# Sums over channels with six blocks added ahead, the gated norm's coefficient on ScalarE, gated blocks in pairs, and a result in four transfers

## The reference, cut to what matters

```
def layer_norm(x, g, b):                     # first block, four times
    mu = mean(x); var = mean(square(x - mu))
    return (x - mu) * rsqrt(var + 1e-5) * g + b

def rmsnorm(u, g):                           # second block
    return u * rsqrt(mean(u * u) + 1e-6) * g

x = layer_norm(ALPHA * x + mix, ln1_g, ln1_b)              # first block
x = layer_norm(ALPHA * x + mlp(x), ln2_g, ln2_b)
xl_new = xl + ml[2] * rmsnorm(y_l, g_post_mix)             # second block, "gated" norm after the mixer
xl_new = xl_new + ml[5] * rmsnorm(mlp_2(h2), g_post_mlp)   # and after the MLP
```

## Time and profile before

| what | value |
| --- | --- |
| median of 3 runs | 1805.22 us (1800.21 to 1808.81) |
| the profiled execution, its own time | 1801.04 us |
| its span, first to last instruction | 1799.2 us |
| outside the span | 1.84 us |
| mean granted TensorE clock | 0.976 |
| TensorE (PE) busy | 1647.6 us, 92% |
| VectorE (DVE) busy | 1190.9 us, 66% |
| ScalarE (ACT) busy | 536.0 us, 30% |
| GpSimd (POOL) busy | 375.8 us, 21% |
| bytes moved | 247.27 MB, mean 137 GB/s |

### The profile page before, as it was taken

How to read it: one execution, slowest core, us unless ns; L and a number is a source line. 1 busy time by engine, 2 the same in 40 slices (tenths; PEclk the granted TensorE clock), 3 DMA queues, 4 the chain that set the end, 5 groups by cost and what they waited for, 6 DMA issues and landing times.

```text
span 1799.2 us, 26861 instructions
## 1 busy us (share of the span) xinstructions
PE 1647.6 (92%) x10914; PEld 1420.9 (79%) x10914; DVE 1190.9 (66%) x1662; ACT 536.0 (30%) x1062; POOL 375.8 (21%) x308
## 2 busy tenths in 40 slices
PE   7978599999899999999888999999999798889996
PEld 6867489999688999988645578888888475679996
DVE  6653478888866888859764464444444687478886
ACT  4424231111353122143465340101011545641111
POOL 1100124444112444400000111212122000134442
PEclk9989899999999999999999999999999899999998
DMA  7850655565656555542201313233333140235551
GB/s 292 296 202 11 235 188 177 187 187 177 235 186 222 176 176 178 180 168 94 82 1 33 132 59 105 90 97 93 98 92 102 37 151 24 70 93 177 176 175 46
DMA packets 69875, 247.27 MB, mean 137 GB/s; under 512 B 7456, under 2 KB 10528, under 8 KB 69664
## 3 DMA queue, kind: packets, MB, share of 16 engines
q1 hardware_dynamic: 69792, 246.18, 42.5%
HBM read 245.10 MB, written 1.05 MB: 137 GB/s over the span
## 4 chain that ended last, share of the span: by engine, by line
PE 64%; DVE 26%; ACT 8%; issue 2%; DMA 1%; SPq 0%; DVEq 0%; ACTq 0%
PE psum L352 14%; PE psum L354 14%; PE psum L353 14%; DVE lo_ring L317 8%; DVE relu L1158 4%; DVE hid_lo L1159 3%; PE psum L368 3%; PE psum L370 2%; PE psum L369 2%; PE psum L988 2%; DVE x L1121 1%; PE psum L451 1%; DVE normed L1119 1%; DVE c_soft L1807 1%; ACT c_p L1628 1%
## 5 line engine op out<-in xcount | busy, mean ns | idle before, releaser
L1965 POOL TENSOR_SCALAR hi_ring<-raw_ring 128x1024 fp32r<-128x1024 f32 x304 | 375.6, 1238 | 1396.5 <-PE psum L354 935.5
L317 DVE TENSOR_TENSOR lo_ring<-raw_ring,hi_ring 128x1024 fp32r<-128x1024 f32 x356 | 535.5, 1505 | 76.1 <-PE psum L354 30.9
L352 PE MATMUL psum<-x_hi,hi_ring 128*128 128x256 f32 (+1 forms) x1360 | 427.7, 315 | 24.9 <-DVE lo_ring L317 13.0
L353 PE MATMUL psum<-x_lo,hi_ring 128*128 128x256 f32 (+1 forms) x1360 | 422.2, 310 | 0.0
L354 PE MATMUL psum<-x_hi,lo_ring 128*128 128x256 f32 (+1 forms) x1360 | 422.1, 310 | 0.0
L352 PE MATMUL psum<-hid_hi,hi_ring 128*128 128x256 f32 (+1 forms) x1024 | 316.8, 309 | 4.1 <-DVE hid_lo L1159 4.1
L354 PE MATMUL psum<-hid_hi,lo_ring 128*128 128x256 f32 (+1 forms) x1024 | 314.6, 307 | 0.0
L353 PE MATMUL psum<-hid_lo,hi_ring 128*128 128x256 f32 (+1 forms) x1024 | 314.0, 307 | 0.0
L352 PEld LDWEIGHTS psum<-x_hi,hi_ring 128*128 128x128 f32 x1360 | 261.2, 192 | 48.8 <-DVE lo_ring L317 18.2
L353 PEld LDWEIGHTS psum<-x_lo,hi_ring 128*128 128x128 f32 x1360 | 261.4, 192 | 13.4 <-issue 0.2
L354 PEld LDWEIGHTS psum<-x_hi,lo_ring 128*128 128x128 f32 x1360 | 261.3, 192 | 13.1
(11 more groups left out here) (376 smaller groups left out, 1962.5 us busy)
## 6 DMA issues: line engine op xcount, KB each, us to landing
raw_ring<-weights SPq DMA_DIRECT2D x460, 512.0 KB, 3.9
h_const<-hyb_consts SPq DMA_DIRECT2D x1, 1088.0 KB, 11.7
x<-xT SPq DMA_DIRECT2D x1, 1024.0 KB, 5.9
x<-ctxT SPq DMA_DIRECT2D x1, 1024.0 KB, 17.1
outT<-x SPq DMA_DIRECT2D x1, 1024.0 KB, 4.8
shared<-shared_consts SPq DMA_DIRECT2D x1, 398.0 KB, 13.8
par<-params SPq DMA_DIRECT2D x1, 301.5 KB, 6.5
```

Of the source, the lines that this page charges most:

```text
L317: nc.vector.tensor_tensor(lo_ring[:, s, :], raw_ring[:, UNIT_AT[u] % RAW_SLOTS, :], hi_ring[:, s, :].bitcast(F32), ALU.subtract).then_inc( ...
L352: nc.tensor.matmul(bank(u % BANKS, T), w_hi, hi[:, k, 0:T], start=(k == 0), stop=False)
L353: nc.tensor.matmul(bank(u % BANKS, T), w_hi, lo[:, k, 0:T], start=False, stop=False)
L1965: nc.gpsimd.tensor_scalar(hi_ring[:, n % SPLIT_SLOTS, :], raw_ring[:, slot, :], 1.0, 0.0, ALU.mult, ALU.add).then_inc(hi_ready, 1)
```

## The change

Five edits. (1) `add_block`: while the last eight units of a stage are drained, VectorE adds blocks 0 to 5 of the tensor that will be summed (`y` for norms 0 to 3, `sq` for norms 5, 7, 9 and 11) into slot 1 of `normed`, one `tensor_tensor` for each of k = 1 to 5; for `sq` it runs one unit later. (2) `added_pe`: TensorE's sum then has three blocks, the added one and blocks 6 and 7, in place of eight (`mean_pe` for the means, `added=True` for the four gated norms). The sums of the other norms are as before. (3) ScalarE multiplies `y` by the gate coefficient: in a mixer it is the scale of the activation that drains PSUM (one for each 256 columns, ahead of the square, and without the link), after an MLP it is an extra activation per 256 columns behind the square. (4) `gated_dve` becomes `normed = y * rstd` and `x = normed + x`, both `tensor_tensor`, over pairs of blocks when T = 256 and over single blocks of 512 columns when T = 512; it also waits for the scaled `y`. (5) The result goes out in four transfers of two blocks, each once its pair is updated.

```diff
--- before.py
+++ after.py
@@ -949,6 +949,8 @@
             nc.vector.scalar_tensor_tensor(y[:, k, 0:SEQ], x[:, k, 0:SEQ], ALPHA, bank(u % BANKS, SEQ), ALU.mult,
                                            ALU.add).then_inc(drained[u % BANKS], 1)
             next_lo(dve, u)
+            wait_drained(dve, u)
+            add_block(dve, link, y, k, SEQ)
 
     def log1p_series(link, e, s, s2, poly):
 
@@ -963,10 +965,7 @@
 
 
     def into_block2_pe(pe):
-        for k in range(KT):
-            wait_drained(pe, U_MLP2 + MLP_UNITS - KT + k)
-            last = nc.tensor.matmul(bank(4, SEQ), ones[:, :], y[:, k, 0:SEQ], start=(k == 0), stop=(k == KT - 1))
-        last.then_inc(flag("mean_ps"), 1)
+        mean_pe(pe, U_MLP2 + MLP_UNITS - KT)
         mods(pe, "mean3")
         context_half(pe, U_L2)
         norm_pe(pe, 3, SEQ)
@@ -975,15 +974,41 @@
         norm_pe(pe, LAYERS[0].norm, SEQ)
         mods(pe, "pre_mix")
 
-    def norm_pe(pe, n, T, mean=None):
+    ADDED = 6
+
+    def added_pe(pe, to, T):
+
+        now["added_pe"] += 1
+        pe.wait_ge(flag("blocks_added"), now["added_pe"])
+        nc.tensor.matmul(to, ones[:, :], normed[:, 1, 0:T], start=True, stop=False)
+
+    def add_block(dve, link, src, k, T):
+
+        part = normed[:, 1, 0:T]
+        if k == 1:
+            link(nc.vector.tensor_tensor(part, src[:, 0, 0:T], src[:, 1, 0:T], ALU.add))
+        elif 1 < k < ADDED - 1:
+            link(nc.vector.tensor_tensor(part, part, src[:, k, 0:T], ALU.add))
+        elif k == ADDED - 1:
+            nc.vector.tensor_tensor(part, part, src[:, k, 0:T], ALU.add).then_inc(flag("blocks_added"), 1)
+
+    now["added_pe"] = 0
+
+    def mean_pe(pe, u):
+        added_pe(pe, bank(4, SEQ), SEQ)
+        for k in range(ADDED, KT):
+            wait_drained(pe, u + k)
+            last = nc.tensor.matmul(bank(4, SEQ), ones[:, :], y[:, k, 0:SEQ], start=False, stop=(k == KT - 1))
+        last.then_inc(flag("mean_ps"), 1)
+
+    def norm_pe(pe, n, T, mean=None, added=False):
 
         if mean:
-            for k in range(KT):
-                wait_drained(pe, mean[1] + k)
-                last = nc.tensor.matmul(bank(4, T), ones[:, :], y[:, k, 0:T], start=(k == 0), stop=(k == KT - 1))
-            last.then_inc(flag("mean_ps"), 1)
+            mean_pe(pe, mean[1])
             mods(pe, f"mean{mean[0]}")
-        for k in range(KT):
+        if added:
+            added_pe(pe, bank(5, T), T)
+        for k in range(ADDED if added else 0, KT):
             pe.wait_ge(flag("norm_sq"), KT * n + k + 1)
             last = nc.tensor.matmul(bank(5, T), ones[:, :], sq[:, k, 0:T], start=(k == 0), stop=(k == KT - 1))
         last.then_inc(flag("norm_sum"), 1)
@@ -1112,15 +1137,17 @@
         dve.wait_ge(flag("norm_rstd"), n + 1)
         scaled_dve(dve, s, T, x, y)
 
-    def gated_dve(dve, link, n, T, l, part):
+    GATED = {SEQ: [(k, k + 2) for k in range(0, KT, 2)], TB: [(k, k + 1) for k in range(KT)]}
+
+    def gated_dve(dve, link, n, T):
 
         dve.wait_ge(flag("norm_rstd"), n + 1)
-        for k in range(KT):
-            link(nc.vector.tensor_tensor(normed[:, k % 2, 0:T], y[:, k, 0:T], rstd[:, 0:T], ALU.mult))
-            for i, c in streams(T):
-                last = nc.vector.scalar_tensor_tensor(x[:, k, c], normed[:, k % 2, c], coef[:, l, part, k, i:i + 1], x[:, k, c],
-                                                      ALU.mult, ALU.add)
-            last.then_inc(flag("x_updated"), 1)
+        dve.wait_ge(flag("y_scaled"), KT * ((n - 3) // 2))
+        for c, (a, b) in enumerate(GATED[T]):
+            t = normed_chunk(c, a, b, T)
+            by = rstd[:, 0:T].unsqueeze(1).broadcast_to([P, b - a, T])
+            link(nc.vector.tensor_tensor(t, y[:, a:b, 0:T], by, ALU.mult))
+            nc.vector.tensor_tensor(x[:, a:b, 0:T], t, x[:, a:b, 0:T], ALU.add).then_inc(flag("x_updated"), b - a)
 
 
     def mlp_pe(pe, m, base, T, s):
@@ -1167,6 +1194,12 @@
                 wait_unit(dve, u)
                 nc.vector.tensor_tensor(y[:, j, 0:T], bank(u % BANKS, T), y[:, j, 0:T], ALU.add).then_inc(drained[u % BANKS], 1)
                 next_lo(dve, u)
+                if i == QUARTERS - 1 and m < 2:
+                    wait_drained(dve, u)
+                    add_block(dve, link, y, j, T)
+                elif i == QUARTERS - 1 and j:
+                    dve.wait_ge(flag("norm_sq"), KT * (3 + 4 * (m - 1)) + j)
+                    add_block(dve, link, sq, j - 1, T)
                 if m == 1 and i in (1, 2) and j % 2 == 0:
                     context_scaled_dve(dve, 4 * (i - 1) + j // 2)
             if m == 1 and i == 2:
@@ -1698,7 +1733,9 @@
         for k in range(KT):
             u = L.base + L2_IN + 3 + k
             wait_unit(act, u)
-            link(nc.scalar.activation(y[:, k, 0:T], bank(u % BANKS, T), ACT.Copy))
+            for i, c in streams(T):
+                last = nc.scalar.activation(y[:, k, c], bank(u % BANKS, T)[:, c], ACT.Identity, scale=coef[:, l, 2, k, i:i + 1])
+            last.then_inc(flag("y_scaled"), 1)
             nc.scalar.activation(sq[:, k, 0:T], bank(u % BANKS, T), ACT.Square).then_inc(flag("norm_sq"), 1)
             act.wait_ge(flag("norm_sq"), KT * (L.norm + 1) + k + 1)
             act.sem_inc(drained[u % BANKS], 1)
@@ -1902,6 +1939,9 @@
             u = L.base + L2_IN + 3 + k
             wait_unit(dve, u)
             next_lo(dve, u)
+            if k:
+                dve.wait_ge(flag("norm_sq"), KT * (L.norm + 1) + k)
+                add_block(dve, link, sq, k - 1, T)
 
     def coef_dve(dve, link, l):
 
@@ -1949,9 +1989,10 @@
 
             for n in range(RAW_SLOTS, len(STREAM)):
                 load(n)
-            sp.wait_ge(flag("x_updated"), KT + 4 * KT)
-            sp.dma_start(out, x[:, :, 0:SEQ]).then_inc(flag("stored"), 16)
-            sp.wait_ge(flag("stored"), 16)
+            for a, b in GATED[SEQ]:
+                sp.wait_ge(flag("x_updated"), 4 * KT + b)
+                sp.dma_start(out[:, a:b, :], x[:, a:b, 0:SEQ]).then_inc(flag("stored"), 16)
+            sp.wait_ge(flag("stored"), 16 * len(GATED[SEQ]))
 
         @block.gpsimd
         def _(pool):
@@ -1999,6 +2040,10 @@
                 for k in range(KT):
                     wait_drained(act, base + MLP_UNITS - KT + k)
                     nc.scalar.activation(sq[:, k, 0:L.T], y[:, k, 0:L.T], ACT.Square).then_inc(flag("norm_sq"), 1)
+                    act.wait_ge(flag("norm_sq"), KT * (L.norm + 3) + k + 1)
+                    for i, c in streams(L.T):
+                        last = nc.scalar.activation(y[:, k, c], y[:, k, c], ACT.Identity, scale=coef[:, L.l, 5, k, i:i + 1])
+                    last.then_inc(flag("y_scaled"), 1)
                 norm_rstd_act(act, link, L.norm + 3, L.T, 1)
 
         @block.vector
@@ -2017,12 +2062,12 @@
             for L in LAYERS:
                 modulated_dve(dve, L.norm, TB if L.l else SEQ, L.split)
                 l2_dve(dve, link, L)
-                gated_dve(dve, link, L.norm + 1, L.T, L.l, 2)
+                gated_dve(dve, link, L.norm + 1, L.T)
                 modulated_dve(dve, L.norm + 2, L.T, L.split + 2)
                 dve.wait_ge(x_ready, KT * (L.split + 4))
                 link(nc.vector.memset(y[:, :, 0:L.T], 0.0))
                 mlp_dve(dve, link, 2 + L.l, L.base + L2_IN + 3 + KT, L.T)
-                gated_dve(dve, link, L.norm + 3, L.T, L.l, 5)
+                gated_dve(dve, link, L.norm + 3, L.T)
 
         @block.tensor
         def _(pe):
@@ -2039,14 +2084,14 @@
                 if L.l:
                     norm_pe(pe, L.norm, TB)
                 l2_pe(pe, L)
-                norm_pe(pe, L.norm + 1, L.T)
+                norm_pe(pe, L.norm + 1, L.T, added=True)
                 if L.l == 0:
                     mods(pe, "post_mix")
                 norm_pe(pe, L.norm + 2, L.T)
                 if L.l == 0:
                     turn_batch(pe, 4)
                 mlp_pe(pe, 2 + L.l, L.base + L2_IN + 3 + KT, L.T, L.split + 2)
-                norm_pe(pe, L.norm + 3, L.T)
+                norm_pe(pe, L.norm + 3, L.T, added=True)
 
 
 
```

## The result

| what | before | after |
| --- | --- | --- |
| median | 1806.22 us (4 runs, 1800.21 to 1808.81) | 1777.78 us (4 runs, 1777.11 to 1778.79) |
| the profiled execution, its own time | 1801.04 us | 1778.79 us |
| its span | 1799.2 us | 1777.0 us |
| mean granted TensorE clock | 0.976 | 0.971 |

The ratio of after to before is 0.9849, with a 95% interval of 0.9826 to 0.9871: faster. One of the runs of before that were taken beside the experiments took 2093.46 us at a granted clock of 0.743, a slower state of the chip, and is left out everywhere. The forecast was 1777.4 us in a range of 1769 to 1791. One number doesn't fit it, though. From profile to profile the span fell by only 1799.2 - 1777.0 = 22.2 us, where the sum said 27.8.

The account below looks back on a forecast made before the run. TensorE was taken as the bound, with 64% of the chain (VectorE 26%, DMA 1%). Means 7.8, gated sums 12.2, gated pass 5.6 and result 2.2 make 27.8 us, taking the 1805.2 us median to 1777.4, range 1769 to 1791.

Parts of the forecast that it names:

- Part 1: Norms 0 to 2: shorter mean sums start centring 1.86 us earlier each, VectorE's last lo part then bounding; 5.6 us.
- Part 2: Norm 3: TensorE reaches the sum of squares 2.16 us earlier and stays the bound; 2.2 us.
- Part 3: Sums of gated norms 5, 7, 9, 11: `stat` earlier by 4.1, 4.3, 1.9 and 1.9 us; 12.2 us.
- Part 4: Gated pass, faster additions and pairs: 1.5, 1.5, 1.1 and 1.5 us at norms 5, 7, 9, 11; 5.6 us.
- Part 5: Result store in four transfers: the last quarter needs 2.6 us where the whole landed in 4.8; 2.2 us.
- Part 6: Forty VectorE additions, 0.42 us each, hidden in 0.59 us idle gaps at no cost; 0.86 us each if contended.
- Additions not hidden: Rival: all forty additions hold up units at 0.86 us each, 34 us, net + 6.6, so 1812; chance 0.03.
- More half clock: Rival: first units behind norms 0 to 3 run at half clock, losing at most 12 us, so 1789; chance 0.06.
- ScalarE's or VectorE's tail: Rival: scaled drains, long lo parts and scaling delay norms, pairs give half; 22 us gained, 1783; chance 0.14.
- Weights at fixed times: Rival: units land when they did, so parts 1 to 3 keep only 8.1 us; 16 us, 1789; chance 0.05.
- Four serial transfers: Rival: result transfers run one after another, norm 11's pass and store gain 0; 24 us left, 1781; chance 0.04.

Follow-up runs that it names:

- TensorE kept at work: Kernel after plus unread extra matmuls in TensorE's waits around norms 6 to 10, against after: 1779.25 us (after 1777.78).

## Why the prediction was right, point by point

**Part 1, the means of norms 0 to 2: right.** Forecast 3 x 1.86 = 5.6 us; the timelines give 1.92 (3.66 - 1.74), 1.90 and 1.76, together 5.58. The next late one is VectorE's last lo part, as forecast.

**Part 2, norm 3: right.** From the mean's start to `stat` it was 11.17 us by the timelines and is 775.43 - 766.42 = 9.01: 2.16 against 2.2.

**Part 3, the gated sums: right within 0.2 us.** 4.30, 4.29, 1.91 and 1.79 make 12.3; forecast 12.2. Oversized was only the scaled drain at norm 5 (1.1 us, measured 0.84), which cost the forecast 0.2 us.

**Part 4, the gated pass: 5.6 forecast, 4.3 measured.** Norms 5 and 7 give 1.45 each for 1.5. Norm 11 gives 1.23 for 1.5: a pair takes 1.40 us and not 1.34, since from a product to its update there are 0.80 us, at norm 5 0.73. The step that failed is norm 9: "before, one block was left after the last update, now two are, 0.43 us more of TensorE, so 1.1 us". It took TensorE at full clock. The stage gave 0.15 us in the first profile of after and 0.32 in the second, and in the one profile of this edit alone it cost 0.52. With TensorE kept at work it gives 9.13 - 8.37 = 0.76. So of the missing 1.0 us 0.4 to 0.6 is the clock (8.98 and 8.81 less 8.37). The rest are sizes, which the timeline with TensorE kept at work gives: the pass is shorter by 1.26 us and not 1.5 (5.68 for 6.94), it starts 0.06 us later behind `rstd`, and squares and sums behind it take 0.44 us more (1.67 for 1.23), much as the forecast had it, though 0.31 of that is the second square of the pair on ScalarE and only 0.13 is TensorE.

**Part 5, the result: right.** 2.36 us in the profile, 2.40 by undoing it, forecast 2.2; a quarter lands in 2.5 us and not 2.6. The section of the Trainium skill that the forecast named (DMA: Bandwidth & Descriptors, Anatomy of one DMA) is about transfers that GpSimd issues. SyncE issues these, so the agreement on the fixed part is no test of it.

**Part 6, the additions: right in sum, wrong in its row.** Alone they change nothing (0.9998). But behind the mixers most additions have a length of 1.26 us (1.53 with 512 columns) and not 0.41, beside GpSimd's copy, while the lo part ahead of it falls from 1.90 to 1.22: together 2.40 us for 1.90, so 0.5 us more and not 0.85. The idle 0.64 us there (before norm 0, timeline of before) took it. The prediction's bound of 0.86 us was too low for the row and too high for the cost. At norm 0 VectorE was late by it: the drain of the unit before the last starts at 246.10 us and that of the last at 247.60, 1.5 us apart where they were 2.88 apart in before, and TensorE didn't wait for it.

**The sum.** 5.6 + 2.2 + 12.3 + 4.3 + 2.4 = 26.8 us by rows, forecast 27.8. The 22.2 us from profile to profile are that, less what else moved in three stages. The start to norm 0 is 3.7 us longer than 252.48 - 1.92, norm 4 to 5 is 2.9 longer than 228.55 - 4.30, and norm 8 to 9 is 2.0 shorter than 163.69 - 1.91: 4.6 together, and 26.8 - 4.6 = 22.2. So of the 5.6 us in question 1.0 is the sizes of terms, and 4.6 is scatter of the kind that two executions of one program show. Norm 8 to 9 warns against reading one column: its 159.81 us stands alone, and all other profiles of after or of kernels built on it have 162.4 to 163.0, before 163.69 and 162.15, so that the 1.9 us of norm 9's sum, plain in its rows, hardly shows in its stage. Between the second profiles the span fell by 1799.3 - 1774.8 = 24.5 us.

The medians fell by 28.4 (1806.22 to 1777.78), 1.6 more than the rows give. The granted clocks account for most of it. Both profiles of before are among its fastest runs, at a mean clock of 0.976 and 0.973, while the 51 runs of before that were taken with the experiments have 0.970 in the mean; the eight runs of after have 0.971, as its profiles. A line through those 51 (1.1 us less for each 0.001 of clock) puts before at 1803.4 us for a clock of 0.972, and one through the eight puts after at 1777.2: by this estimate 26.2 us at equal clock. So it is partly luck that 1777.4 was forecast and 1777.8 measured: the sum was 1.0 us too large and its base 1.0 us too low (1805.2 for 1806.2), and the medians happened to lie 1.6 us further apart than the rows.

**The rivals.** Additions not hidden: refuted. More half clock: not shown. Within the span TensorE is at half clock for 88 and 96 us in the profiles of before, 104 and 98 in those of after, but 109 with the additions alone, so that is scatter; behind norms 0 to 2, where the forecast put it, the stages kept their gain. At norm 9 the half clock was there before, and the shorter pass of pairs made it count (0.4 to 0.6 us). ScalarE's or VectorE's tail: the pairs did give less, 4.3 for 5.6, and nothing else of it showed. Weights at fixed times: refuted, the stages from norm 0 to 1 and from 1 to 2 are 1.93 and 1.64 us shorter, so the gain at norms 1 and 2 reached them. Four serial transfers: refuted.
